# Reordering the opening, the routing stage and the last experts of a two-block transformer kernel on one Trainium2 core

## The chip, the cores and the metric

The kernel runs on one core of a Trainium2 chip. The core has five engines with queues of their own: TensorE (PE, matrix products into the eight PSUM banks), VectorE (DVE), ScalarE (ACT), GpSimd (POOL) and SyncE (SP, which here only issues DMAs). Sixteen DMA engines move data between HBM and the on-chip SBUF. Engines wait for each other through semaphores only. The metric is the device time of one execution in microseconds, lower is better.

## The reference, cut to what matters

Everything is float32. Two blocks run one after the other on 256 tokens (`x`) of width 1024; the first also carries 256 context tokens.

```python
# first block, layer 0 (gated linear attention), layer 1 (neighbourhood attention)
for i in range(2):
    mod = silu(c) @ ada_w[i] + ada_b[i]              # shifts, scales, gates
    h = rms_norm(x, g1) * (1 + s1) + sh1
    x = x + g1 * mixer(h)                            # gla_mixer or na_mixer
    h = rms_norm(x, g2) * (1 + s2) + sh2
    a, val = split(h @ w_in)                         # 1024 -> 2 * 2816
    x = x + g2 * ((silu(conv3(a)) * val) @ w_out)    # 2816 -> 1024
x = rms_norm(x, final_g)
# second block: 16 meta tokens in front of the 256
p = rms_norm(h) @ w_in_2
h = h + concat(hyena(p), hgrn2(p)) @ w_out_2
a = rms_norm(h, norm_ffn)
group = argmax(a @ w_rg); e1, e2 = top2(softmax(a @ w_re[group]))      # 64 experts
h = h + sum(gate_e * (silu(a @ w_gate[e]) * (a @ w_up[e])) @ w_down[e])
return rms_norm(h, norm_final)[16:]
```

An expert's three matrices (`w_gate`, `w_up`: 1024 x 512, `w_down`: 512 x 1024) are 2 MB each, 192 matrices in all, and the kernel reads them all.

## The kernel before, in words

**First block.** Activations lie transposed: `xT`, `hT` hold 8 chunks of 128 channels by 512 tokens (256 of them in layer 1). Weights come as slabs of 2 MB through a ring of four slots (`ring`), in an order written out in `first_block_slabs`; SP issues them one by one, each as soon as the count on the semaphore of its slot's last reader is there. The large products are split for precision: a float32 operand is rounded to the fast format `fp32r` by ACT ("hi"), DVE subtracts to get the rest ("lo"), and `split_mm` (L692 to L696) makes three fast products hi*hi, hi*lo and lo*hi in place of one plain float32 product. So each half slab passes ACT (`..._hi`), then DVE (`..._lo`, counted on `w_lo`), before PE may use it; each activation chunk passes the same way (`h_hi`, `h_lo`; in the second half of a feed-forward network `f_hi`, `f_lo`).

**Opening.** PE makes the norm's sum, then `ada_rows(0)`, `ada_rows(1)` (products of the conditioning vector with a slab of `ada_w`, 64 instructions with the four-column layout of `ada_products`), turns them (`ada_turn`) and begins the first projection: `unit(u, chunks)` adds some of the eight chunks of output tile `u`. Chunks 0 to 3 can be done once half of the modulation is known; chunks 4 to 7 need `ada_rows(2)`, `ada_rows(3)` and their turns, then DVE's `columns(1)` and ACT's `modulate`. The order on PE is: `unit(0)`, `unit(1)` with chunks 0, 1, 2; `ada_rows(2)`; chunk 3; `ada_rows(3)`; turn 2; part of `unit(2)`; turn 3; and so on. DVE does eight `factors`, then `rest(0)` and the lo half of the first weights, which POOL has rounded.

**Feed-forward, layer 1.** `ffn(l, T)` exists on PE, ACT and DVE. For 22 tiles `i` PE makes 48 products (two output halves of eight chunks, three products each). ACT rounds the weights of tile `i + 2`, does the convolution's middle tap and, after DVE's `taps`, the silu; DVE subtracts for tile `i + 2`, does the taps and the final product into `f_act`. After the loop 22 chunks of `f_act` are rounded (`ffn_out_prepared`) and subtracted (`act_rest`), the first two ahead of the rest, and eight output tiles `m` of 66 products follow, each with a slab rounded by `ffn_w_out_hi` / `ffn_w_out_lo`.

**Routing.** PE makes the logits and turns the token rows (`logits_and_rows`), waits for DVE's chain of some 25 small steps (group, two experts, ranks), makes the ranks' products (L1379 to L1382), gathers the tokens of the first expert (`gather_first`) and starts expert 0.

**Experts.** Each of the 64 experts gets 32 token slots. `expert(e)` on PE: `gate_up` (32 products of 256 columns, four side by side), a turn of the hidden tile, `down` (16 products). ACT applies silu and copies, DVE multiplies. The experts go in groups of four (`GE`); `gather` fills 128 slots for the next group, and `combine(g)` adds a finished group's rows to `z_tok`, which holds the residual, with four products of 128 x 512 and four DVE additions. `load(n)` on SP issues matrix `n` (gate, up, down of expert `n // 3`) into one of eight homes (`e_slot`) once the last reader of the home is through: for `n >= 8` the count on `gu_mm` or `down_mm`. Matrices 0 to 7 go as soon as `first_free` allows: 0 and 1 long before, 2 to 5 in the last transforms, 6 and 7 at `proj_mm` 28 and 32. Matrix 8 (`NINTH`) and matrix 9 (`TENTH`) lie in scattered free tiles (8 and 11 parts of 256 or 128 KB), after 7 in the queue. Matrices 10 and 11 share homes with 0 and 1 and are issued in quarters as expert 0's `gate_up` passes (`GU_PART`).

**The end.** After expert 63: `combine(15)`, four additions, per half of the tokens a square with a sum, Ln and Exp for the root, one DVE product with the gain, one store.

## Time and profile before

| | |
|---|---|
| runs, us | 2356.7, 2358.27, 2360.92 (median 2358.27) |
| profiled execution, us | 2357.33, of which the span from the first to the last instruction is 2355.5 |
| busy, share of the span | PE 83%, PE weight loads 62%, DVE 40%, ACT 29%, POOL 4% |
| DMA engines | 592 MB, mean 251 GB/s |
| mean granted PE clock | 0.931 of full speed |

Times in the profile are from the first instruction. A busy PE is one with a product under way, at whatever clock: the granted clock has a full level (1.00) and a half one (0.50), and a number between them is a stretch with both. A matmul in float32 that is not `fp32r` shows as two records.

### The profile page before, as it was taken

The numbers are of one execution on the slowest core, as the hardware profiler recorded it, in microseconds if no ns is written. First come the engines' busy times: TensorE is split into PE (matmuls) and PEld (weight loads), VectorE is DVE, ScalarE is ACT, GpSimd is POOL, SyncE is SP. The second block draws the span as 40 slices with busy tenths as digits, with TensorE's granted clock in tenths as the row PEclk, the third lists the DMA queues.
The fourth block names the chain that finished last, engine by engine and source line by source line (L and its number), as shares of the span: only waits on it lengthen the run. The fifth ranks groups of instructions, "written<-read, shape, count | busy, mean of one in ns | idle before, by whom it ended". The sixth has DMA issues, their size and how long they took to land.

```text
span 2355.5 us, 38024 instructions
## 1 busy us (share of the span) xinstructions
PE 1943.9 (83%) x16576; PEld 1463.5 (62%) x16576; DVE 935.4 (40%) x1636; ACT 691.0 (29%) x1255; POOL 94.2 (4%) x112
## 2 busy tenths in 40 slices
PE   5999899999999999999899998666666566666665
PEld 4896567888787887998896465433333343333332
DVE  3346745344424246665666374332111121111112
ACT  4333435322414246544553323111111111111111
POOL 0010110000001011000200000000000000000000
PEclk9999999999999999999999998888888888888888
DMA  6306462221225224444530349999999999999996
GB/s 274 144 36 245 186 250 108 107 96 61 77 107 223 108 71 173 176 162 147 215 119 10 137 198 373 426 428 427 427 427 426 428 426 427 426 428 426 427 427 279
DMA packets 47861, 592.27 MB, mean 251 GB/s; under 512 B 5917, under 2 KB 6873, under 8 KB 12240
## 3 DMA queue, kind: packets, MB, share of 16 engines
q1 hardware_dynamic: 44272, 580.21, 60.1%
q0 software_dynamic: 2992, 8.57, 1.2%
q8 instruction: 132, 2.16, 0.4%
q10 hardware_dynamic: 432, 1.06, 0.1%
q14 instruction: 33, 0.27, 0.0%
HBM read 588.77 MB, written 1.05 MB: 250 GB/s over the span
## 4 chain that ended last, share of the span: by engine, by line
PE 46%; DMA 27%; DVE 8%; ACT 5%; issue 2%; POOL 0%; SPq 0%; ACTq 0%; DVEq 0%; POOLq 0%
DMA s_ring<-in_w_up 14%; PE bank L694 9%; PE bank L696 9%; PE bank L695 9%; DMA s_arena<-in_w_up 6%; PE bank L1407 6%; DMA s_hT<-in_w_up 4%; DVE s_ring_r L2243 3%; ACT s_arena_r L1572 3%; DMA s_xT<-in_w_up 3%; PE bank L1439 2%; PE bank L1394 1%; PE bank L1445 1%; PE bank L1229 1%; ACT s_arena L1572 1%
## 5 line engine op out<-in xcount | busy, mean ns | idle before, releaser
L694 PE MATMUL bank<-s_arena_r 128*128 128x256 f32 (+2 forms) x1816 | 592.1, 326 | 24.4 <-DVE s_hT_r L2248 9.3
L696 PE MATMUL bank<-s_arena_r,s_ring_r 128*128 128x512 f32 (+2 forms) x1472 | 489.4, 332 | 0.0
L1572 ACT ACTIVATE s_arena<-bank 32x256 f32<-32x256 f32 (+6 forms) x418 | 167.5, 407 | 1025.9 <-PE bank L1407 552.8
L1407 PE MATMUL bank<-s_ring,s_arena 128*32 128x256 f32 x1984 | 279.4, 496 | 150.5 <-DMA s_hT<-in_w_up 39.6
L695 PE MATMUL bank<-s_hT_r,s_arena_r 128*128 128x512 f32 (+2 forms) x1144 | 385.1, 337 | 0.0
L694 PEld LDWEIGHTS bank<-s_arena_r 128*128 128x128 f32 x1816 | 341.2, 188 | 60.9 <-issue 13.8
L2243 DVE TENSOR_TENSOR s_ring_r<-s_ring,s_arena_r 128x2048 fp32r<-128x2048 f32 (+3 forms) x121 | 251.0, 2085 | 277.2 <-ACT s_arena_r L1572 277.0
L696 PEld LDWEIGHTS bank<-s_arena_r,s_ring_r 128*128 128x128 f32 x1472 | 278.1, 189 | 29.1
L1407 PEld LDWEIGHTS bank<-s_ring,s_arena 128*32 128x32 f32 x1984 | 135.9, 141 | 226.4 <-issue 213.9
L1572 ACT ACTIVATE s_arena_r<-s_ring 128x2048 fp32r<-128x2048 f32 (+3 forms) x121 | 208.8, 1737 | 153.3 <-PE bank L696 123.5
L2926 DVE TENSOR_TENSOR s_arena<-s_arena,bank 64x256 f32<-64x256 f32 x64 | 27.1, 423 | 522.3 <-ACT s_arena L1572 522.3
L695 PEld LDWEIGHTS bank<-s_hT_r,s_arena_r 128*128 128x128 f32 x1144 | 216.0, 189 | 24.3 <-issue 0.5
L1407 PE MATMUL bank<-s_arena 128*32 128x256 f32 x1084 | 120.4, 491 | 55.3 <-DMA s_arena<-in_w_up 37.4
L695 PE MATMUL bank<-s_arena_r 128*128 128x256 f32 (+1 forms) x464 | 150.8, 325 | 0.0
L695 PE MATMUL bank<-s_ring_r,s_arena_r 128*128 128x256 f32 (+1 forms) x464 | 130.1, 280 | 0.0
L1572 ACT ACTIVATE s_arena<-s_arena 128x512 f32<-128x512 f32 (+7 forms) x176 | 86.3, 529 | 140.2 <-DVE s_arena L2236 98.5
L1407 PE MATMUL bank<-s_hT,s_arena 128*32 128x256 f32 x544 | 92.9, 516 | 38.5 <-DMA s_ring<-in_w_up 38.5
L1407 PEld LDWEIGHTS bank<-s_arena 128*32 128x32 f32 x1084 | 62.3, 140 | 90.2 <-issue 80.7
L2984 DVE COPY s_arena<-bank 32x256 f32<-32x256 f32 x128 | 54.3, 425 | 152.1 <-PE bank L1439 149.6
L696 PE MATMUL bank<-s_arena_r,s_hT_r 128*128 128x256 f32 (+1 forms) x336 | 94.3, 281 | 0.0
L1407 PE MATMUL bank<-s_xT,s_arena 128*32 128x256 f32 x480 | 77.1, 492 | 19.6 <-DMA s_ring<-in_w_up 19.6
L695 PEld LDWEIGHTS bank<-s_arena_r 128*128 128x128 f32 x464 | 88.0, 190 | 7.3
(366 smaller groups left out, 2530.6 us busy)
## 6 DMA issues: line engine op xcount, KB each, us to landing
s_ring<-in_slabs SPq DMA_DIRECT2D x68, 2048.0 KB, 8.6
s_ring<-in_w_down SPq DMA_DIRECT2D x32, 2048.0 KB, 28.5
s_ring<-in_w_up SPq DMA_DIRECT2D x32, 2048.0 KB, 33.3
s_ring<-in_w_gate SPq DMA_DIRECT2D x30, 2048.0 KB, 33.3
s_arena<-in_w_gate SPq DMA_DIRECT2D x16, 2048.0 KB, 33.3
s_arena<-in_w_up SPq DMA_DIRECT2D x16, 2048.0 KB, 33.3
s_arena<-in_w_down SPq DMA_DIRECT2D x14, 2048.0 KB, 29.5
s_ring<-in_slabs SPq DMA_DIRECT2D x16, 1408.0 KB, 6.2
```

The lines of the kernel that those rows point to most:

```text
L694: mm(out, w_hi_, x_hi_, start=start, stop=False, skip_group_check=skip)
L695: mm(out, w_hi_, x_lo_, start=False, stop=False, skip_group_check=skip)
L696: return mm(out, w_lo_, x_hi_, start=False, stop=stop, skip_group_check=skip)
L1229: last = mm(bank[:, :], dft_w(i, kt, r0=r), (f_hs if i < 2 else f_hd)[rows, od, kt, :], start=a == 0, stop=a == 2, skip_group_check=True)
L1394: last = mm(pb[6 + hf][:, P * c:P * c + n], r_h2[:, i, 512 * hf + P * c:512 * hf + P * c + P], r_S[:, buf, i, 0:n], start=i == 0, stop=i = ...
L1407: last = mm(pb[b][32 * q:32 * q + 32, 0:256], x[:, c, :], (gate, up)[q // 2](c, q % 2), start=c == 0, stop=c == DC - 1, skip_group_check=True)
L1439: last = mm(pb[3 + b][32 * q:32 * q + 32, 0:256], e_hT[:, b, 64 * a + 32 * half_:64 * a + 32 * half_ + 32], w(2 * half_ + a, q), start=a + ...
L1445: return mm(pb[(5, 6, 7, 5)[k]][:, :], r_SgT[0:n, buf, P * i:P * i + P], y_g[0:n, buf, 512 * hf:512 * hf + 512], start=True, stop=True)
L1572: return act.activation(out, in_, func, **kw)
L2243: TTn(view_r, view, hi.bitcast(F32), ALU.subtract).then_inc(S["w_lo"], 1)
L2926: return TTn(e_hid[0:64, b, :], e_sg[0:64, b, :], pb[b][64:128, 0:256], ALU.mult)
L2984: dve.tensor_copy(y_g[32 * j:32 * j + 32, g % 2, 256 * q:256 * q + 256], pb[3 + b][32 * q:32 * q + 32, 0:256]).then_inc(S["y_dve"], 1)
```

## The change

Seven edits, in the order of the kernel.

1. **Opening.** On PE `ada_rows(2)` stands ahead of the first `unit`, `ada_rows(3)` after chunk 1, the turns after chunk 2 and 3. On DVE the lo half of the first weights stands ahead of `rest(0)`, and the last two `factors` between the rests.
2. **Feed-forward of layer 1.** The first output tile is one plain float32 product per chunk. Its chunks' hi and lo parts, for the other seven tiles, are made inside the loop of 22 (`act_rounded(i - 1)` on ACT, `act_rest(i - 2)` on DVE), in places of their own.
3. **Second block's first projection.** DVE's `half_lo(2)` stands ahead of the eight products into `zT`.
4. **Products that nobody reads** (`idle_products`, plain float32, 128 x 512): five after `ffn(1)`, five ahead of the wait for the routing (`route_M`), one after the ranks' products.
5. **Loads.** SP issues six parts of matrix 8 and two narrow ones of matrix 9 ahead of matrices 6 and 7; the first half of matrix 10 goes whole into `z_tok`, and its second half into its home.
6. **Residual.** `z_tok` is therefore not filled by ACT; the first `combined` takes the residual from `r_h2`, scaled back by `n_root`, which costs one DVE reciprocal. PE's wait for `n_act` 13 goes.
7. **Last experts.** Expert 62 runs as before; ahead of it PE puts the residual and the rows of experts 60 and 61 into four banks. Expert 63's gate and up products are 128 columns wide in 4 x 8 pieces per matrix, its up and down matrices come in halves of 1 MB with semaphores of their own, its hidden tile needs one turn. The rows of experts 62 and 63 are added by products of 32 rows (`own_rows`). Then ACT squares and DVE multiplies by the gain straight from the banks, both halves of the tokens share one Ln and one Exp, ACT scales one half, DVE the other, and both stores start together.

```diff
@@ first_block_slabs / f_hi
+            if T == NT:
+                return f_lo[:, c, NT:TT]
+        def f_rest(c, T):
+            if T == TT:
+                return f_lo[:, c, 0:T]
+            return (hT_r, xT_r, h_hi)[c // DC][:, c % DC, NT:TT]
@@ sync
+            for n in range(6):
+                load(n)
+            sp.wait_ge(S["hyena_y"], HC)
+            for i in range(6):
+                ninth_part(i)
+            narrow_part(1)
+            narrow_part(3)
+            load(6)
+            load(7)
+            sp.wait_ge(S["z_pe"], Z_ROWS(DC))
+            for i in range(6, 8):
+                ninth_part(i)
+            for i, home in enumerate(tenth_wide):
+                tenth_part(home, 512 * i)
+            narrow_part(0)
+            narrow_part(2)
+            n = TENTH + 1
+            sp.dma_start(eleventh_half, weights[n % 3][n // 3, :, 0:2048]).then_inc(S["slab_in4"], 16)
+            sp.wait_ge(S["z_set"], DC + 1)
+            for i in range(4, 6):
+                narrow_part(i)
...
                 if n == TENTH + 1:
                     for k in range(4):
-                        for i in range(2):
+                        for i in range(0 if k >= 2 else 1, 2):
...
+                if n in LAST_HALVES:
+                    sp.dma_start(e_slot[s][:, 0:2048], weights[n % 3][n // 3, :, 0:2048]).then_inc(S[LAST_HALVES[n][0]], 16)
+                    sp.dma_start(e_slot[s][:, 2048:4096], weights[n % 3][n // 3, :, 2048:4096]).then_inc(S[e_in[s][0]], 16)
+                    return
@@ tensor: ffn(l, T, norm)
+                    if m == 0 and l:
+                        w = got(out_slab(l, m))
+                        for c in range(FC):
+                            pe.wait_ge(S["ffn_act"], FC * l + c + 1)
+                            last = mm(pb[2][:, 0:T], w[:, c, :], f_act[:, c, 0:T], start=c == 0, stop=c == FC - 1)
+                        last.then_inc(S["ffn_out_mm"], 1)
+                        continue
...
+            def idle_products(bank, moving, n):
+                for _ in range(n):
+                    mm(bank[:, :], ident, moving, start=True, stop=True)
@@ tensor: opening
-            for c in range(3):
+            ada_rows(2)
+            for c in range(2):
                 unit(0, [c])
                 unit(1, [c])
-            ada_rows(2)
+            ada_rows(3)
+            unit(0, [2])
+            unit(1, [2])
+            ada_turn(2)
             unit(0, [3])
             unit(1, [3])
-            ada_rows(3)
-            ada_turn(2)
-            unit(2, range(2))
             ada_turn(3)
-            unit(2, range(2, 4))
+            unit(2, range(4))
             unit(3, range(4))
...
             ffn(1, NT, "fin")
+            idle_products(pb[0], ka[:, :], 5)
...
+            pe.wait_ge(S["route_in"], 48)
+            idle_products(pb[3], gain_out[:, 0:512], 5)
             pe.wait_ge(S["route_M"], 1)
...
+            idle_products(pb[3], gain_out[:, 0:512], 1)
...
-                pe.wait_ge(S["n_act"], 13)
@@ tensor: last_experts
+                for k, (i, hf) in enumerate(TH):
+                    mm(z_bank[k][:, :], ident, z_tok[:, i, 512 * hf:512 * hf + 512], start=True, stop=False, skip_group_check=True)
+                for k, (i, hf) in enumerate(TH):
+                    mm(z_bank[k][:, :], r_SgT[0:P - 64, 1, P * i:P * i + P], y_g[0:P - 64, 1, 512 * hf:512 * hf + 512], start=False, stop=False, skip_group_check=True)
+                expert(e - 1)
+                quarters(pb[0], arrived(3 * e), range(DC)).then_inc(S["gu_mm"], 1)
+                own_rows(0)
+                quarters(pb[3], first_half(3 * e + 1), range(4))
+                quarters(pb[3], arrived(3 * e + 1), range(4, DC)).then_inc(S["gu_mm"], 1)
+                pe.transpose(pb[2][:, 0:P], e_hid[:, 1, 0:P], ident).then_inc(S["hid_tr"], 1)
+                w = first_half(3 * e + 2)
+                for c in range(4):
+                    if c == 2:
+                        arrived(3 * e + 2)
+                    for q in range(4):
+                        last = mm(pb[4][32 * q:32 * q + 32, 0:256], e_hT[:, 1, 32 * c:32 * c + 32], w[:, D * c + 256 * q:D * c + 256 * q + 256], start=c == 0,
+                                  stop=c == 3, skip_group_check=True)
+                own_rows(1)
@@ scalar
-                    if i == FC - 1:
+                    if i == FC - 1 and l == 0:
                         ffn_w_out_hi(l, 0)
                         for c in range(2):
                             A(f_hi(c, T), f_act[:, c, 0:T], ACT.Copy).then_inc(S["f_hi"], 1)
+                    if l and i >= 1:
+                        act_rounded(i - 1)
-            for i in range(2):
-                for hf in range(2):
-                    A(z_tok[:, i, 512 * hf:512 * hf + 512], z_rows[i][hf][:, :], ACT.Copy).then_inc(S["n_act"], 1)
+                for k in range(4):
+                    act.wait_ge(S["comb_mm"], 4 * NGRP + 8 + k + 1)
+                    if k == 2:
+                        act.wait_ge(S["z_add"], 4 * (NGRP - 1) + 2)
+                    A(z_tok[:, i, 512 * hf:512 * hf + 512], z_bank[k][:, :], ACT.Square, accum_out=n_acc[:, 1, k:k + 1]).then_inc(S["n_act"], 1)
+                A(n_rstd[:, 1, :], n_rstd[:, 1, :], ACT.Ln, bias=eps[:, 0:1], scale=1.0 / D).then_inc(S["n_act"], 1)
+                A(n_rstd[:, 1, :], n_rstd[:, 1, :], ACT.Exp, scale=-0.5).then_inc(S["n_act"], 1)
+                A(r_h2[:, 1, :], r_h2[:, 1, :], ACT.Copy, scale=n_rstd[:, 1, 1:2]).then_inc(S["n_act"], 1)
@@ vector
+                    if l and i >= 2:
+                        act_rest(i - 2)
...
             factors(0, 6)
             columns(0)
-            factors(6, 2)
+            gla_w_in_lo(0)
+            rest(0)
+            rest(1)
+            factors(6, 1)
+            rest(2)
+            factors(7, 1)
+            rest(3)
...
             half_lo(1, "in2")
+            half_lo(2, "in2")
...
+                dve.wait_ge(S["n_act"], 9)
+                step(dve.reciprocal(n_root, n_rstd[:, 0, :]))
...
+                for k in (2, 3, 0, 1):
+                    TTn(r_h2[:, i, 512 * hf:512 * hf + 512], z_bank[k][:, :], gain_out[:, 512 * hf:512 * hf + 512], ALU.mult).then_inc(S["z_add"], 1)
+                TTn(n_rstd[:, 1, :], n_acc[:, 1, 0:4:2], n_acc[:, 1, 1:4:2], ALU.add).then_inc(S["z_add"], 1)
+                TS(r_h2[:, 0, :], r_h2[:, 0, :], n_rstd[:, 1, 0:1], None, ALU.mult).then_inc(S["out_set"], 1)
```

## Rows read from the trace of the kernel before

**Rows 1.** The page: GB/s in 40 slices, and the chain by engine.

```profile
GB/s 274 144 36 245 186 250 108 107 96 61 77 107 223 108 71 173 176 162 147 215 119 10 137 198 373 426 428 427 427 427 426 428 426 427 426 428 426 427 427 279
PE 46%; DMA 27%; DVE 8%; ACT 5%; issue 2%; POOL 0%; SPq 0%; ACTq 0%; DVEq 0%; POOLq 0%
```

**Rows 2.** Timeline, opening: start us, length us, engine, line, operation, count, idle before.

```profile
24.66 4.66 POOL L594 CAST s_arena_r<-s_ring 128x2048 fp32r<-128x2048 f32 x2 [23.16 <-DMA s_ring<-in_slabs]
...
32.95 0.79 PE L694 MATMUL bank<-s_arena_r 128*128 128x512 f32 x1 [7.93 <-DVE s_ring_r L2329]
...
39.83 1.95 PE L770 MATMUL bank<-s_ring,s_ones 128*32 128x128 f32 x64
...
46.74 0.27 PE L785 MATMUL bank<-s_ka,s_arena 128*128 128x128 f32 x1
```

**Rows 3.** PE's windows, opening: stretch, length, busy (count), granted clock, DMA share, GB/s.

```profile
38.00:40.00 2.00, 2.00 (x16) 0.89 1.00 426
```

**Rows 4.** Timeline, feed-forward of layer 1, all engines.

```profile
1061.30 1.90 ACT L1572 ACTIVATE s_arena_r<-s_ring 128x2048 fp32r<-128x2048 f32 x1
...
1063.23 2.29 DVE L2243 TENSOR_TENSOR s_ring_r<-s_ring,s_arena_r 128x2048 fp32r<-128x2048 f32 x1 [1.39 <-ACT s_arena_r L1572]
...
1076.88 2.77 DVE L2266 TENSOR_TENSOR s_arena_r<-s_arena,s_hT_r 128x256 fp32r<-128x256 f32 x8
...
1074.07 0.28 PE L696 MATMUL bank<-s_arena_r,s_ring_r 128*128 128x256 f32 x1
...
1088.28 0.39 PE L694 MATMUL bank<-s_arena_r 128*128 128x256 f32 x1 [3.61 <-DVE s_ring_r L2243]
```

**Rows 5.** PE's windows, in that loop and behind its stall.

```profile
1000.00:1055.00 55.00, 55.00 (x470) 1.00 0.46 167
...
1090.00:1092.00 2.00, 2.00 (x12) 0.50 0.02 6
```

**Rows 6.** Start of the second block's first projection: timeline, then chain (start, length).

```profile
1153.92 0.57 PE L694 MATMUL bank<-s_arena_r 128*128 128x272 f32 x1 [5.06 <-DVE s_hT_r L2248]
...
1168.68 0.51 DVE s_arena L2236
```

**Rows 7.** Timeline, routing and expert 0, PE and SP.

```profile
1424.08 0.79 PE L1379 MATMUL bank<-s_arena,s_ka 128*128 128x128 f32 x2 [5.07 <-DVE s_arena L2860]
...
1427.37 1.94 PE L1453 MATMUL bank<-s_arena 128*32 128x256 f32 x16 [1.32 <-DVE s_arena L2899]
...
1431.08 5.33 PE L1407 MATMUL bank<-s_arena 128*32 128x256 f32 x64 [0.54 <-ACT s_arena L1572]
...
1441.13 1.94 PE L1439 MATMUL bank<-s_ring,s_arena 128*32 128x256 f32 x32 [0.47 <-ACT s_arena L1572]
...
1443.11 0.33 SPq L560 DMA_DIRECT2D s_ring<-in_w_gate  x1
```

**Rows 8.** PE's windows of 1 us in the routing, columns as in rows 3.

```profile
1415.00:1416.00 1.00, 1.00 (x9) 1.00 0.00 0
...
1433.00:1434.00 1.00, 1.00 (x14) 0.50 0.35 121
```

**Rows 9.** PE's windows of 1 us near the end.

```profile
2319.00:2320.00 1.00, 0.29 (x4) 0.50 1.04 442
...
2331.00:2332.00 1.00, 0.00 (x0) 1.00 0.57 229
```

**Rows 10.** Timeline, the last two experts and the end.

```profile
2311.98 1.93 PE L1439 MATMUL bank<-s_ring,s_arena 128*32 128x256 f32 x32 [0.41 <-issue]
...
2334.35 0.64 PE L1407 MATMUL bank<-s_hT,s_arena 128*32 128x256 f32 x2 [4.57 <-DMA s_ring<-in_w_up]
...
2344.98 3.67 PE L1445 MATMUL bank<-s_arena 128*128 128x512 f32 x8 [1.04 <-ACT s_arena L1572]
...
2348.69 0.69 DVE L2931 TENSOR_TENSOR s_arena<-s_arena,bank 128x512 f32<-128x512 f32 x1 [0.17 <-PE bank L1445]
...
2352.47 0.36 ACTq L2174 DMA_DIRECT2D out_y<-s_arena  x1
```

More of the change, by code:

```diff
@@ L451, in build @@
         e_in = [(f"slab_in{e_ring[i]}", count[e_ring[i]]) if i in e_ring else (f"expert_in{i}", 0) for i in range(NSLOT)]
+        N_ACT = 9
+        z_bank = [pb[k] for k in (6, 7, 1, 5)]
+        own_y = [y_g[:, 0, 256 * k:256 * k + 256] for k in range(2)]
+        own_SgT = [r_SgT[:, 0, :], r_S[:, 0, :, :].rearrange("p a n -> p (a n)")]
         sems = S
@@ L1551, in _ @@
                     pe.wait_ge(S["x_done"], j + 2)
-            for e in range(GE * MIDDLE, NE):
+            for e in range(GE * MIDDLE, NE - 2):
                 expert(e)
-            combine(NGRP - 1)
+            last_experts()
         @block.scalar
```

197 lines of the change are left out of this document (142 added, 55 removed).

## The prediction

> **What bounds the kernel now.** I read the page first, then the chain of waits, then windows and timelines of the stages that the change touches. The page's GB/s line [rows 1] splits the kernel in two. Up to slice 23 (some 1390 us) the DMA rate changes from slice to slice and the chain by engine is mostly PE (46% of the span): compute is the bound. From slice 25 on the rate stands at 426 to 428 GB/s to the end: the matrices of the experts stream in, and a matrix of 2.097 MB costs 4.9 us however fast the engines are (DMA is 27% of the chain, all of it there). So a microsecond counts in four places: ahead of the stream it moves the stream's start; in the routing it counts if DMA engines have run dry; between the experts it counts nothing; behind the last matrix it counts in full.
>
> **1. Opening.** PE sits idle 7.93 us before its first projection product at 32.95 [rows 2], and the clock comes back to the full level only inside 38 to 40 (0.89) [rows 3]; the first product took 0.79 us. The turn whose result gates chunks 4 to 7 starts at 46.74 [rows 2]. The change puts `ada_rows(2)` in the hole. When is its slab there? POOL's cast, released by the third slab, starts at 24.66 [rows 2]; the fourth lands one slab later, 24.7 + 4.9 = 29.6. At half clock the 64 products take twice the 1.95 us of [rows 2], to 33.5, by when DVE has the first lo half (cast half done at 27.0, plus 2.3 [rows 4], and behind POOL's second cast, 29.3 + 2.3 = 31.6, at worst). PE works from 29.6 instead of 32.95 (3.3 us), and starts its way to full clock as much earlier: some 3.4 us less at half speed give 1.7 us. Chunks 5 and on still wait for the ACT and DVE steps behind turn 3, which move with it, so about 0.3 is lost: **4.7 us**. Bounds: 0 (the wait comes back behind the turn) and 6.5 (clock back at once).
>
> **2. Feed-forward of layer 1.** Before: the loop's last product starts at 1074.07, and the second output tile starts at 1088.28 after a wait of 3.61 us for the lo half of its weights, [rows 4]; the clock then drops to 0.50 for 3.4 us [rows 5], worth 1.7. New: behind the loop stand 22 plain products of 256 columns. The nearest row is the combine, 3.67 us for four of 512 columns plus tail [rows 10], thus 0.43 to 0.46 each, 9.7 us in all. The cover for the second tile's weights (ACT 1.90 and DVE 2.29 for 2048 columns [rows 4], so 2.6 and 3.1 for 2816) is then these 9.7 us. If the loop is as long as before, tile 1 starts at 1074.2 + 9.7 = 1083.9, a gain of 4.4.
> But the loop gets a longer chain. ACT's rounding (1.90), DVE's subtraction (2.29, starting 1.9 after it) [rows 4], the taps, the silu and the return to ACT make a ring of 5.5 us per tile (1.9 + 2.3 + two taps of 0.5, [rows 6], + 0.3). PE needs 48 x 55/470 = 5.62 [rows 5], only 0.1 more. `act_rest(i - 2)` stands in this ring between the subtraction and the taps and costs 2.77 / 8 = 0.35 [rows 4]; 17 tiles of it are 5.9 us. ACT's extra rounding lies beside DVE's subtraction and is free. The cover: tile 21's lo half is ready at 1063.23 + 2.29 = 1065.5, PE needs it at 1074.2 - 5.6 = 1068.6, so 3.1 us are spare and PE slips by 5.9 - 3.1 = 2.8. Gain: 4.4 - 2.8 + 1.7 (no stall, no clock drop) = **3.3 us**. Bounds: 6.1 (no slip), and -2 (ACT's step of the same size in the ring too).
>
> **3. Second block's projection.** The unread products (5 x 0.86 = 4.3 us by [rows 10]) lie in a wait of 5.06 us [rows 6]. PE then begins at full clock, but is paced by DVE's h_lo, and the fifth tile waits for DVE's taps of the first (second tap at 1168.68, [rows 6]). Moving `half_lo(2)` ahead of the eight products leaves the taps behind the same sum of DVE work. **0**; bounds -1 (a product at half clock sticks out) and +1.4.
>
> **4. Routing and loads.** Before: DMA ran dry at 1415 (0 GB/s) and partly at 1433 (121) [rows 8], because matrices 6 and 7 wait for PE and the quarters of 10 and 11 for expert 0. The first free-running matrix, 12, is issued at 1443.11 [rows 7], when expert 0's `down` is through; by then what was queued is just delivered. From issue to flow lie some 1.7 us: matrix 12 starts to arrive at 1444.8.
> New: the parts of 8 and 9 (1.8 MB, 4.3 us) fill the time behind matrix 5; half of 10 (2.5 us) fills the hole before the quarters. All twelve matrices are in some 2 us before matrix 12 can flow (the three megabytes left of 10 and 11 take 7.4 us from about 1431.6 on). But then matrix 12 decides, which waits for `down_mm` 1, so what counts is how much sooner PE is through with expert 0. PE waits 5.07 us for DVE's routing chain [rows 7], during which the clock goes to half and stays there at 1433 [rows 8]. Five products (4.3 us at full clock, from 1419.0 to 1423.3) lie in that wait with 0.8 to spare. With the clock held, the ranks' product (0.79) saves 0.3, the gather (1.94) 1.0, the turn 0.25, expert 0's 5.33 goes to 8 x 0.43 = 3.4 (four columns of 256 side by side, the combine's rate in [rows 10]), 1.9; the 4.7 us from there to its `down` were at full clock already [rows 7]. Sum 3.45, so **3.5 us**: matrix 12 at 1439.6 instead of 1443.1, its data flowing from 1441.3 instead of 1444.8. The reciprocal (0.2) lies beside PE's gathers. Bounds: if the clock drops all the same but after the five, 0.5; if it drops under them (5 x 1.7 = 8.5 us, 3.4 more than the wait), -3.1; 6 if PE gives more.
>
> **5. Last experts.** Before: matrix 190 (up) releases PE at 2334.35, at half clock after 4.57 us idle; `combine` starts at 2344.98, the last addition at 2348.69, the last store at 2352.47, and the end is 3.0 us behind it [rows 10]. New: gate products of expert 63 are done while 190 lands; of 190 only half a matrix of products is left (0.9 to 1.7 us). Matrix 191's second half lands 4.9 us after 190, at 2339.2, and is now what ends last. From there: 8 of 16 down products 1.0, copy 0.45, eight products of 32 rows in two turns 1.3, a ladder of ACT squares and DVE products on two banks each 2.8 (4 x 0.69 [rows 10]), sum, Ln and Exp 0.8, scaling 1.2: 2346.8. Then 3.0 and, as both 0.5 MB stores start together, 1.2 more (0.5 MB at the 427 GB/s of [rows 1]): 2351.0. Against 2355.5: **4.5 us**. Bounds: 2 (32-row products one after the other, 8 x 0.43) and 6 (stores beside each other, squares closer).
> By the Trainium skill, "DMA: Bandwidth & Descriptors", section "Issuing engines are not separate DMA queues", DMAs started by two engines end up on the same 16 engines and interleave. The row for one store shows 3.0 us to the end; no row has two together. By that rule the 1.2 stand; without it the sum would be 1.2 better.
> The extra work ahead of expert 62 (16 small and 8 large products, 8 us) starts at 2313.9, and expert 62's matrix lets PE start at 2319.7 [rows 9, 10]: 2.5 us late, but then at full clock. Its cover is the wait for 190; were it gone (all at half clock) the end would move by up to 2 us.
>
> **Sum.** 4.7 + 3.3 + 0 + 3.5 + 4.5 = 16.0. The profiled execution took 2357.33 us (span 2355.5 and 1.8 around it), which is 0.9 below the median of the runs, 2358.27. 2357.33 - 16.0 = 2341.3; with half of that difference added, I say **2341.8**.
>
> **Rivals.**
> A. *The clock is not held in the routing.* Between the products PE still has four waits of 0.5 to 1.3 us [rows 7]. For: the clock was at half through all such waits before. Against: it had fallen in the long one ahead. Time: item 4 at 0.5 or -3.1, thus 2344.8 to 2348.4. The Trainium skill, "TensorE: Matmul & The Clock Gate", section "A second HAM failure mode: psum-queue depth-cycling", says that short idle stretches between groups of matmuls make the clock swing; by it this rival comes true. The trace shows the granted clock at 1.00 at 2331 after a `down` with waits around it [rows 9], which speaks against it.
> B. *The ring of layer 1 does not reach PE,* or half as much: 2339.0. For: no PE wait in the loop [rows 5]. Against: the spare time counted above.
> C. *Tail or opening give half:* 32-row products in series, or PE waiting again behind the third turn. 2344.2.
> D. *Slower.* In the last 12 us the engines move only 229 GB/s [rows 9]: about half of the sixteen are through and half are behind by some 12 us in a stream of 950 us, and the late half sets every landing. If parts with short rows in a new order, or the halves, put more on the late half, the stream itself stretches. It decides from 16/950 = 1.7%; at 2% it costs 19 us: 2361. For: the lag exists. Against: all changed transfers together are under 10 MB of 403, and rate in all slices is the same.
> E. *The front's gain is eaten* by a wait in the attention stages: only items 4 and 5 count, 2349.8.
>
> **How the numbers follow.** Forecast 0.47, A 0.20, B 0.12, C 0.10, D 0.05, E 0.06. A change of 0.2% (4.7 us) is about what a measurement of this kernel can tell: faster means below 2353.6. All but D are there; for errors in several items at once I take some off: faster 0.88, same 0.07, slower 0.05. The range reaches to A and B with their bounds: 2334 to 2350.
>
> **What would show it.** PE's `ada_rows(2)` at 29 to 30 and turn 3 near 42; in layer 1 small PE waits for lo halves from about tile 9 on, and tile 1 without the 3.61 us wait; PE clock 1.00 at 1420 to 1430; matrix 12 issued 3 to 4 us earlier relative to the routing; the last store issued some 8 us behind the last matrix's landing instead of 13. Wrong if turn 3 moves and the scan does not, or if the slices from 25 on show less than 426 GB/s.

## The result and the profile after

| | before | after |
|---|---|---|
| median of the runs shown side by side, us | 2356.81 (2354.54 to 2360.92) | 2342.97 (2340.68 to 2348.44) |
| ratio | | 0.9942, 95% interval 0.9933 to 0.9952 |
| profiled execution, us | 2357.33 | 2340.68 |
| its span, us | 2355.5 | 2338.9 |
| mean granted clock | 0.931 | 0.938 |

The forecast was 2341.8 us, in a range of 2334 to 2350. The interval lies clear of 1: the kernel is faster by 0.6%. The gain itself is known less well than the table suggests. The span of the profiled execution is 16.6 us shorter, where the sum of the five terms said 16.0, but that execution was the fastest of its six; the two medians lie 13.8 us apart, and in the sets of runs below the changed kernel is 17.9 and 16.2 us ahead.

The page of the changed kernel, the GB/s line and the chain by engine, answers to [rows 1]:

```profile
GB/s 276 145 37 261 183 241 109 108 103 55 78 108 224 110 69 176 158 167 163 207 129 10 125 207 394 426 427 427 428 426 427 427 426 427 428 426 427 427 427 311
PE 48%; DMA 29%; DVE 6%; ACT 4%; issue 2%; POOL 0%; SPq 0%; DVEq 0%; ACTq 0%; POOLq 0%
```

The shape is the same: compute up to slice 23, the stream of expert matrices at 426 to 428 GB/s from slice 25 on. The slice between them rose from 373 to 394 GB/s. So the stream did not stretch (rival D); it starts earlier, has fewer holes at its start, and less comes behind it.

**Opening.** Timeline of the changed kernel (start us, length us, engine, line, operation, count, idle before), against [rows 2]:

```profile
24.43 4.16 POOL L625 CAST s_arena_r<-s_ring 128x2048 fp32r<-128x2048 f32 x2 [22.93 <-DMA s_ring<-in_slabs]
26.79 3.94 DVE L2492 TENSOR_TENSOR s_ring_r<-s_ring,s_arena_r 128x2048 fp32r<-128x2048 f32 x1
30.55 3.64 PE L812 MATMUL bank<-s_ring,s_ones 128*32 128x128 f32 x64 [5.95 <-DMA s_ring<-in_slabs]
34.12 0.61 PE L725 MATMUL bank<-s_arena_r 128*128 128x512 f32 x1
37.19 1.95 PE L812 MATMUL bank<-s_ring,s_ones 128*32 128x128 f32 x64
42.06 0.27 PE L827 MATMUL bank<-s_ka,s_arena 128*128 128x128 f32 x1
```

`ada_rows(2)` fills the hole, at half clock (3.64 us; its twin at 37.19 takes 1.95), and turn 3 (`ada_turn(3)`, the one that gates chunks 4 to 7) stands at 42.06 where it was at 46.74. The slab landed 0.9 us later than I had it. DVE's lo half takes 3.94 us beside POOL's cast; the same operation takes 2.28 us at 34.40, where POOL is idle.

**Feed-forward of layer 1 and the projection behind it**, against [rows 4] and [rows 6]:

```profile
1064.26 2.29 DVE L2399 TENSOR_TENSOR s_ring_r<-s_ring,s_arena_r 128x2048 fp32r<-128x2048 f32 x1 [1.39 <-ACT s_arena_r L1690]
1066.47 0.42 DVE L2422 TENSOR_TENSOR s_arena_r<-s_arena,s_arena_r 128x256 fp32r<-128x256 f32 x1
1072.37 9.66 PE L763 MATMUL bank<-s_arena,s_ring 128*128 128x256 f32 x44
1140.62 4.45 PE L784 MATMUL bank<-s_ka 128*128 128x512 f32 x10
1145.84 0.36 PE L725 MATMUL bank<-s_arena_r 128*128 128x272 f32 x1 [0.76 <-DVE s_hT_r L2404]
1153.73 0.40 PE L725 MATMUL bank<-s_arena_r 128*128 128x272 f32 x1 [1.64 <-DVE s_ring_r L2399]
```

The plain tile takes 9.66 us (22 products, recorded as 44), the wait of 3.61 us behind it is gone. The projection begins 8.08 us earlier than in [rows 6], 4.65 of which the opening gave.

**Routing**, against [rows 7]:

```profile
1410.78 0.34 PE L1420 MATMUL bank<-s_ka,s_arena 72*128 72x72 f32 x2 [0.25 <-ACT s_arena L1690]
1410.96 4.50 PE L784 MATMUL bank<-s_arena,s_ka 128*128 128x512 f32 x10
1416.18 0.49 PE L1425 MATMUL bank<-s_arena,s_ka 128*128 128x128 f32 x2 [0.72 <-DVE s_arena L3025]
1421.50 3.66 PE L1454 MATMUL bank<-s_arena 128*32 128x256 f32 x64 [0.43 <-ACT s_arena L1690]
1422.62 1.19 SPq L546 DMA_DIRECT2D s_arena<-in_w_down  x2
1431.86 0.33 SPq L561 DMA_DIRECT2D s_ring<-in_w_gate  x1
```

Windows of it, against [rows 8] (stretch, its length, busy us of PE, PEld, DVE, ACT, POOL, granted clock, DMA share, GB/s):

```profile
1407.00:1408.00 1.00, 1.00 (x10) 0.93 (x10) 0.03 (x1) 0.00 (x0) 0.00 (x0) 1.00 1.03 442
1425.00:1426.00 1.00, 1.00 (x12) 0.91 (x9) 0.97 (x4) 0.38 (x1) 0.00 (x0) 1.00 1.01 356
```

The two stretches that stood at 0 and 121 GB/s carry 442 and 356, the clock is full, expert 0's gate and up products take 3.66 us instead of 5.33, and matrix 12 is issued 21.08 us behind the 72 x 72 turn instead of 24.44. The first of the quarters of matrices 10 and 11 (the row of L546) is issued 11.84 us behind it.

**The end**, against [rows 10]:

```profile
2325.38 1.07 PE L1633 MATMUL bank<-s_xT,s_arena 128*32 128x256 f32 x16 [0.46 <-ACT s_arena L1690]
2327.04 1.07 PE L1633 MATMUL bank<-s_xT,s_arena 128*32 128x256 f32 x16 [0.59 <-DMA s_xT<-in_w_down]
2328.71 1.56 PE L1604 MATMUL bank<-s_arena 32*128 32x256 f32 x16 [0.60 <-ACT s_arena L1690]
2330.38 2.57 DVE L3235 TENSOR_TENSOR s_arena<-bank,s_arena 128x512 f32<-128x512 f32 x4 [1.77 <-PE bank L1604]
2333.82 0.75 DVE L3239 TENSOR_SCALAR s_arena<-s_arena 128x1024 f32<-128x1024 f32 x1 [0.60 <-ACT s_arena L1690]
2334.99 0.37 ACTq L2330 DMA_DIRECT2D out_y<-s_arena  x1
```

Only half of the down products (1.07 us) are left when the last bytes arrive, and the last store is issued 8 us behind that release. By the trace's DMA records the last packet of the weights ends at 2326.55, 8.4 us ahead of the last store and 12.3 us ahead of the end; in the kernel before it ended at 2338.66, 13.8 us and 16.9 us ahead of them.

### The profile page after: what moved, and what is told of

Read it like the earlier page. It is cut to its first block, busy times and chain, and to the rows that moved or that the text cites. A ratio compares the mean times of both kernels' runs of the same rounds, so it can differ in the third digit from the quotient of the medians.

```text
span 2338.9 us, 38292 instructions
## 1 busy us (share of the span) xinstructions
PE 1953.3 (84%) x16711; PEld 1466.6 (63%) x16711; DVE 929.9 (40%) x1634; ACT 687.8 (29%) x1253; POOL 93.7 (4%) x112
## 4 chain that ended last, share of the span: by engine, by line
PE 48%; DMA 29%; DVE 6%; ACT 4%; issue 2%; POOL 0%; SPq 0%; DVEq 0%; ACTq 0%; POOLq 0%
DMA s_ring<-in_w_up 14%; PE bank L725 10%; PE bank L727 10%; PE bank L726 10%; DMA s_arena<-in_w_up 6%; PE bank L1454 5%; DMA s_xT<-in_w_up 4%; DMA s_hT<-in_w_up 3%; DVE s_ring_r L2399 2%; ACT s_arena_r L1690 2%; PE bank L1490 2%; DMA s_xT<-in_w_down 1%; PE bank L1441 1%; PE bank L1273 1%; PE bank L1496 1%
## 5 line engine op out<-in xcount | busy, mean ns | idle before, releaser
L725 PE MATMUL bank<-s_arena_r 128*128 128x256 f32 (+2 forms) x1858 | 603.5, 325 | 8.5 <-DVE s_hT_r L2404 3.9
L727 PE MATMUL bank<-s_arena_r,s_ring_r 128*128 128x256 f32 (+2 forms) x1514 | 499.4, 330 | 0.0
L726 PE MATMUL bank<-s_hT_r,s_arena_r 128*128 128x512 f32 (+2 forms) x1200 | 398.9, 332 | 0.0
L1454 PE MATMUL bank<-s_ring,s_arena 128*32 128x256 f32 x1952 | 272.3, 494 | 146.9 <-DMA s_hT<-in_w_up 39.4
L725 PEld LDWEIGHTS bank<-s_arena_r 128*128 128x128 f32 x1858 | 347.6, 187 | 46.4 <-issue 9.1
L726 PEld LDWEIGHTS bank<-s_hT_r,s_arena_r 128*128 128x128 f32 x1200 | 225.0, 188 | 24.2 <-issue 0.5
L1690 ACT ACTIVATE s_arena<-s_arena 128x512 f32<-128x512 f32 (+6 forms) x174 | 85.1, 527 | 137.9 <-DVE s_arena L2392 96.0
L1454 PE MATMUL bank<-s_hT,s_arena 128*32 128x256 f32 x512 | 85.9, 509 | 34.3 <-DMA s_ring<-in_w_up 34.3
L726 PE MATMUL bank<-s_arena_r 128*128 128x512 f32 (+1 forms) x330 | 112.5, 341 | 0.0
L726 PEld LDWEIGHTS bank<-s_ring_r,s_arena_r 128*128 128x128 f32 (+1 forms) x464 | 85.9, 185 | 0.5
```

What stands on the lines that cost most here:

```text
L725: mm(out, w_hi_, x_hi_, start=start, stop=False, skip_group_check=skip)
L726: mm(out, w_hi_, x_lo_, start=False, stop=False, skip_group_check=skip)
L727: return mm(out, w_lo_, x_hi_, start=False, stop=stop, skip_group_check=skip)
L1454: last = mm(pb[b][32 * q:32 * q + 32, 0:256], x[:, c, :], (gate, up)[q // 2](c, q % 2), start=c == 0, stop=c == DC - 1, skip_group_check=True)
L1690: return act.activation(out, in_, func, **kw)
```

## The experiments

The kernels ran in three sets, each on a chip of its own and beside runs of the kernel before. Sets 1 and 3 hold the changed kernel too, as a yardstick. Set 2 (residual ahead, opening held, old end, old opening) has none, and "above the yardsticks" there compares runs on different chips; the medians of the kernel before were 2359.09, 2356.70 and 2357.65 us in the three sets. Times are medians of five. Single executions of one kernel lie up to 8 us apart (2340.68 to 2348.44 for the changed kernel), and the intervals of most kernels overlap that of the yardstick, so a difference of 2 or 3 us between two medians decides nothing alone. I read each verdict from lengths of stages inside the traces as well, one trace per kernel:

| kernel | median us | ratio to before, interval | turn 3 | norm sum | to projection | turn 72x72 to matrix 12 | to last half |
|---|---|---|---|---|---|---|---|
| changed, set 1 | 2341.24 | 0.9932 (0.9919 to 0.9946) | 41.47 | 938.18 | 206.81 | 21.10 | 915.47 |
| changed, set 3 | 2341.50 | 0.9934 (0.9920 to 0.9948) | 41.94 | 938.82 | 206.82 | 21.09 | 916.63 |
| no products in routing | 2345.34 | 0.9942 (0.9929 to 0.9956) | 43.06 | 937.95 | 206.91 | 24.50 | 921.18 |
| old loads | 2344.49 | 0.9942 (0.9929 to 0.9956) | 41.85 | 938.16 | 207.43 | 21.09 | 918.48 |
| neither | 2346.30 | 0.9953 (0.9940 to 0.9967) | 41.63 | 938.48 | 206.87 | 24.47 | 920.65 |
| residual ahead | 2338.70 | 0.9929 (0.9915 to 0.9942) | 42.12 | 937.71 | 204.57 | 21.09 | 916.31 |
| opening held | 2341.53 | 0.9935 (0.9921 to 0.9948) | 40.07 | 936.23 | 206.80 | 21.09 | 918.03 |
| old end | 2345.04 | 0.9947 (0.9934 to 0.9961) | 41.70 | 938.37 | 206.89 | 21.09 | |
| old opening | 2347.67 | 0.9964 (0.9950 to 0.9977) | 46.87 | 943.64 | 206.89 | 21.09 | 916.57 |
| old feed-forward | 2345.57 | 0.9951 (0.9938 to 0.9965) | 42.15 | 937.51 | 210.24 | 21.08 | 916.37 |
| item 3 off | 2341.56 | 0.9938 (0.9925 to 0.9952) | 41.71 | 938.49 | 206.83 | 21.09 | 916.12 |
| both gains | 2336.71 | 0.9913 (0.9900 to 0.9927) | 40.10 | 934.81 | 203.95 | 21.09 | 915.95 |

"Turn 3" is the start of `ada_turn(3)` in the opening, "norm sum" the start of PE's sum ahead of the second block's feed-forward, "to projection" the time from there to the first product of the second block's projection, "to last half" from PE's 72 x 72 turn in the routing to the product that the last matrix's second half releases (the old end has no halves). All lengths are in us.

### The changed kernel as yardstick (two runs)

No edit.

> The changed kernel itself, unedited, as the yardstick for the runs beside it. Every theory: 2341 to 2346 us, 14 to 16 us under the kernel before.

> The changed kernel itself once more, as the yardstick of the three runs beside it. Every theory: 2340 to 2345 us.

Measured: 2341.24 and 2341.50 us.

### No products in the routing

```diff
-            pe.wait_ge(S["route_in"], 48)
-            idle_products(pb[3], gain_out[:, 0:512], 5)
...
-            idle_products(pb[3], gain_out[:, 0:512], 1)
```

> The six unread products in the routing are left out (five behind the group product, one ahead of the first expert), all loads stay as changed. Theory T (the routing part of the gain needs PE's clock held, because PE's last products there say when the quarters of matrices 11 and 12 and later matrix 12 may be issued): the granted clock falls from 1.00 to 0.50 in about 1418 to 1424, matrix 12 is issued 2.5 to 3.7 us later than in the changed kernel (1431.9), and the kernel takes 2 to 4 us more. Rival (DMA alone counts, the early loads give all of it): within 0.7 us of the changed kernel.

Measured: 2345.34 us, 4.1 above the yardstick. Timeline and two windows of this kernel:

```profile
1415.01 0.80 PE L1423 MATMUL bank<-s_arena,s_ka 128*128 128x128 f32 x2 [5.07 <-DVE s_arena L3022]
1421.89 5.49 PE L1451 MATMUL bank<-s_arena 128*32 128x256 f32 x64 [0.43 <-ACT s_arena L1687]
1423.88 2.04 SPq L546 DMA_DIRECT2D s_arena<-in_w_down  x2
1434.09 0.33 SPq L561 DMA_DIRECT2D s_ring<-in_w_gate  x1
```

```profile
1419.00:1420.00 1.00, 1.00 (x12) 0.20 (x4) 0.18 (x1) 0.00 (x0) 0.00 (x0) 0.50 1.15 450
1424.00:1425.00 1.00, 1.00 (x16) 0.61 (x12) 0.86 (x6) 0.00 (x0) 0.00 (x0) 0.50 0.55 94
```

The wait of 5.07 us of [rows 7] is back, the clock stands at 0.50 behind it, and expert 0's gate and up products take 5.49 us (5.33 in [rows 7], 3.66 in the changed kernel). Behind the turn the first quarter is issued 2.5 us later (14.29 us) and matrix 12 3.4 us later (24.50), and as the early loads are then through, the queues run low (94 GB/s). The rival, that DMA alone gives the gain, is out.

### Loads in the old order

```diff
-            for n in range(6):
+            for n in range(8):
                 load(n)
...
-            n = TENTH + 1
-            sp.dma_start(eleventh_half, weights[n % 3][n // 3, :, 0:2048]).then_inc(S["slab_in4"], 16)
```

The counts of the waits, the four quarters of the eleventh matrix and `up` of expert 3 go with it.

> The six products stay; the loads go back to the order of before (matrices 6 and 7 ahead of the ninth's and tenth's parts, no half of the eleventh in the residual's buffer, four quarters of it into its slot). Theory T (early loads are needed too, since otherwise the queues run dry and the stream is short of 1 MB when PE could go on): the DMA share falls to about 0 for 1 to 2 us near 1407, PE waits for the eleventh or twelfth matrix, and the kernel takes 1.5 to 3.5 us more than the changed one. Rival H (the clock alone is the gain, the bytes were there in any case): within 0.7 us of the changed kernel.

Measured: 2344.49 us, 3.3 above. Window of this kernel:

```profile
1407.00:1408.00 1.00, 1.00 (x9) 0.85 (x9) 0.26 (x1) 0.00 (x0) 0.00 (x0) 1.00 0.00 0
```

Matrix 12 is issued at the same 21.09 us behind the turn as in the changed kernel, and still 1.8 us of the stream are lost (counted in bytes, below): the dry microseconds can't be made up. The rival "clock alone" is out. My expectation had PE waiting for the eleventh or twelfth matrix; no such wait exists. The lost bytes come out only at the end of the stream. The median's 3.3 is more than the loss: in the profiled execution of this kernel the work behind the last bytes took 14.2 us and not 12.3, with its last products at half clock (see the last section); some kernels with the new loads show the same.

### Neither

Both edits together.

> Both left out: no products held in the routing and the loads in the order of before. Theory T (two conditions, of which the later one counts): 3 to 4.5 us more than the changed kernel, clearly less than the sum of what the two single edits cost if each of these costs over 2 us. Rival S (the two gains add): the sum of the two single edits' costs, 5 us or more.

Measured: 2346.30 us, 5.1 above, a little more than I expected; the two single costs sum to 7.4. To count it inside the traces I took the bytes of the 69 us that start exactly 34 us ahead of the 72 x 72 turn, and set them against 427 GB/s. (The start must be exact: nothing flows there yet, so a window that starts 0.4 us earlier counts 0.4 us more as lost.) Time lost: changed kernel 7.5 (set 1), 7.7 (set 3) and 7.9 us; no products 11.8; old loads 9.5; neither 12.1; kernel before 12.2. Against the mean of the changed kernel, 7.7, the single edits cost 4.1 and 1.8, both together 4.4, and the routing term is worth 4.3 us between the two profiled executions of before and after. From there to 2303 us the stream loses 0.1 to 0.4 us in all of them. It's two conditions of which the later one counts; they don't add: with the new loads the products are worth 4.1 us, with the old ones 2.6, and the loads alone 0.3. "Neither" still has item 6, which no run takes out; the kernel before, without it, loses the same.

### Activation residual ahead of the weight's

```diff
+                    if l and i >= 2:
+                        act_rest(i - 2)
                     if i + 2 < FC:
                         ffn_w_in_lo(l, i + 2)
...
-                    if l and i >= 2:
-                        act_rest(i - 2)
```

> In the second block's feed-forward loop VectorE makes the activation's residual of two chunks ago ahead of the weight's residual instead of behind it, in the 1.39 us that it idles there. Theory R (the ring of VectorE and ScalarE sets the period of 5.83 us, because the 0.44 us of residual stand behind the wait): the period goes back to 5.5, the first plain product stands 2 to 3 us earlier than the 1072.5 of the changed kernel, and the kernel is 2 to 3.2 us faster. Rival P (PE sets the period, or the residual delays the weight's residual that PE needs): within 0.7 us.

Measured: 2338.70 us. That is 2.7 below the yardsticks, but they belong to other sets; against the kernel before beside it the ratio is 0.9929, where the yardsticks have 0.9932 and 0.9934, which would be 1 us. So the median does not decide, and the stage does. Timeline of this kernel, the last tile of the loop with a weight's residual:

```profile
1056.43 0.42 DVE L2422 TENSOR_TENSOR s_arena_r<-s_arena,s_arena_r 128x256 fp32r<-128x256 f32 x1
1057.90 2.29 DVE L2399 TENSOR_TENSOR s_ring_r<-s_ring,s_arena_r 128x2048 fp32r<-128x2048 f32 x1 [1.05 <-ACT s_arena_r L1690]
1068.79 9.66 PE L763 MATMUL bank<-s_arena,s_ring 128*128 128x256 f32 x44
```

The residual stands in DVE's idle time now. DVE's weight residuals follow each other every 5.50 us, as in the kernel before, and not every 5.83 us as in the changed kernel. From the norm sum to the plain tile it is 131.1 us instead of 133.3, and 130.5 in the kernel with both gains, where no clock drop falls in the loop's start. PE counts 469 matmul records in 1000 to 1055, against 454 in the changed kernel and 470 in [rows 5]: the ring no longer reaches PE. The slip that the prediction put at 2.8 us is 2.2 to 2.8. The expectation holds, rival P is out.

### Products in the opening's wait

```diff
+            idle_products(pb[3], ka[:, 0:512], 6)
             ada_rows(2)
```

> Six unread products of 128x512 (0.89 us each at full clock) stand in the opening in PE's 5.95 us wait for the slab, ahead of the adaLN group's product. Theory (a granted clock of 0.50 in 28 to 34 costs that group 3.64 instead of 1.95 us): clock 1.00 throughout 24 to 36, the group takes 1.95 us, turn 3 at about 40.4 instead of 42.1, and the kernel is 1.2 to 1.9 us faster. Rival (behind the group PE waits for ScalarE and VectorE, which are busy in 26 to 34): the first product of the unit stays near 34.1, and nothing or under 0.5 us is gained. Other rival: the six products end behind the slab's landing and cost their overhang, up to 0.5 us slower.

Measured: 2341.53 us. Timeline of this kernel:

```profile
24.64 5.32 PE L784 MATMUL bank<-s_ka 128*128 128x512 f32 x12
30.26 1.96 PE L812 MATMUL bank<-s_ring,s_ones 128*32 128x128 f32 x64 [0.31 <-DMA s_ring<-in_slabs]
40.07 0.27 PE L827 MATMUL bank<-s_ka,s_arena 128*128 128x128 f32 x1
```

The opening does what the theory says: turn 3 comes 1.4 to 1.9 us sooner, and the routing 2.0 to 2.6 us. The time does not show it. In the profiled execution the engines trickle on at 0.02 to 0.24 of their share in the last 4 us of the stream, the last half is released 1.4 to 2.6 us late, and its products run at half clock (1.93 us instead of 1.07), with 14.2 us from the last bytes to the end instead of 12.3. By itself this run is inconclusive.

### The end as before

Everything that item 7 adds is taken out: `expert(62)`, `expert(63)`, `combine(15)`, the old additions, squares and scaling.

```diff
-            for e in range(GE * MIDDLE, NE - 2):
+            for e in range(GE * MIDDLE, NE):
                 expert(e)
-            last_experts()
+            combine(NGRP - 1)
```

> Everything of the change but the last two experts, which run as before: no halves of the last two matrices, products of 32 rows for all, combination of 128 rows after the last down product, squares and scaling after the additions. The term of the prediction: 4.5 us (2 to 6) slower than the changed kernel, 17 us or more from the last byte of the weights to the end of the span against 12.9. Rival (the end of the stream comes later by itself, the tail is hidden by the lag of some DMA engines): under 2 us.

Measured: 2345.04 us, 3.7 above the mean of the yardsticks. The span is 2343.9 us and the last packet of the weights ends at 2326.96, so 16.9 us lie behind it, as in the kernel before, against 12.3 in the changed kernel (2338.9 and 2326.55). The difference is 4.6 us. Windows of both, first the changed kernel, then this one, and the timeline of this one:

```profile
2326.50:2327.00 0.50, 0.00 (x0) 0.00 (x0) 0.00 (x0) 0.00 (x0) 0.00 (x0) 1.00 0.00 0
2326.50:2327.00 0.50, 0.50 (x12) 0.30 (x8) 0.00 (x0) 0.00 (x0) 0.00 (x0) 0.50 0.00 0
```

```profile
2333.36 3.67 PE L1491 MATMUL bank<-s_arena 128*128 128x512 f32 x8 [1.04 <-ACT s_arena L1619]
2337.07 0.69 DVE L2999 TENSOR_TENSOR s_arena<-s_arena,bank 128x512 f32<-128x512 f32 x1 [0.17 <-PE bank L1491]
```

The two long steps of [rows 10] are back with the same lengths. The rival is out. Five of the twelve traces with the new end have the last products at half clock and 14.2 us behind the last bytes; against those the new end is worth 2.7 us and not 4.6.

### The opening as before

The order of PE and DVE of before:

```diff
-            ada_rows(2)
-            for c in range(2):
+            for c in range(3):
                 unit(0, [c])
                 unit(1, [c])
-            ada_rows(3)
...
+            ada_rows(2)
```

> Everything of the change but the order of the opening stage, which is the order of before on PE and VectorE. The term of the prediction: turn 3 back at 46.7, kept to the end, 4.7 us (3.5 to 5.5) slower than the changed kernel. Rival E (a later stage takes part of a gain at the front): under 3 us slower.

Measured: 2347.67 us, 6.3 above the yardsticks. Turn 3 at 46.87, the norm sum at 943.64, as in the kernel before (46.74, 943.71); against the yardsticks 4.8 to 5.5 us. It's the largest term, and kept to the end. Rival E is out. The median's 6.3 is above my 5.5; in this profiled execution the last half of the stream is released 4.9 to 6.7 us later than in the yardsticks, so the rest is scatter of the executions and of the sets as far as I can tell.

### The second feed-forward as before

The plain tile, the rounding in the loop and the places of the residuals are taken out, for `l` = 1 all runs as for `l` = 0.

```diff
-                    if m == 0 and l:
-                        w = got(out_slab(l, m))
...
-                    if l and i >= 2:
-                        act_rest(i - 2)
```

> Everything of the change but the second block's feed-forward, which is made as before (first output tile with three products per chunk, activation rounded behind the loop). The term of the prediction: from the norm sum ahead of the loop to the second block's projection 3.3 us longer than in the changed kernel, with PE waiting 3.6 us before the second tile and the clock at 0.50 beside it, and the kernel 3.3 us (2.5 to 4.5) slower. Rival (the slip of the ring and the plain tile cancel): under 1.5 us slower.

Measured: 2345.57 us, 4.1 above; 210.24 to the projection, 3.4 more. Timeline and window of this kernel:

```profile
1082.10 0.38 PE L721 MATMUL bank<-s_arena_r 128*128 128x256 f32 x1 [3.61 <-DVE s_ring_r L2382]
```

```profile
1084.00:1086.00 2.00, 2.00 (x11) 2.00 (x11) 1.44 (x2) 0.53 (x2) 0.00 (x0) 0.50 0.00 0
```

The wait of 3.61 us is back to the hundredth and the clock stands at 0.50 behind it: the term's 3.3 us. The rival is out.

### Item 3 off

```diff
-            idle_products(pb[0], ka[:, :], 5)
...
-            half_lo(2, "in2")
```

> Left out: the five unread products behind the second feed-forward; and the weight's residual 2 of the input projection is made inside its loop again, as before. The prediction puts this item at nothing (-1 to 1.4): within 0.7 us of the changed kernel, although the granted clock may stand at 0.50 for some us near 1140 to 1146. Rival: a projection tile at half clock moves all behind it, 0.7 to 1.5 us slower.

Measured: 2341.56 us, the same as the yardsticks, and 206.83 to the projection. Timeline and window of this kernel:

```profile
1145.32 0.56 PE L725 MATMUL bank<-s_arena_r 128*128 128x272 f32 x1 [5.05 <-DVE s_hT_r L2403]
```

```profile
1147.00:1149.00 2.00, 2.00 (x11) 2.00 (x10) 2.00 (x7) 1.27 (x4) 0.00 (x0) 0.50 0.00 0
```

The projection starts at half clock, as before the change, and nothing is later for it: from the norm sum to the 72 x 72 turn of the routing it is 471.63 us, and 471.59 in the yardstick. In the changed kernel PE's next wait there, at 1153.73, is for DVE. The rival is out.

### Both gains

The edits of "residual ahead" and "opening held" in one kernel.

> The changed kernel with both edits that helped one by one: VectorE's activation residual ahead of the weight's residual, and six unread products in PE's opening wait. If the two lie in stages of their own, the gains add: the routing starts 2.5 + 2 = 4.5 us earlier than in the changed kernel, and the time is 3.5 to 5 us below it, about 2338 us. Rival (the stream of weights starts at a fixed time or ends no earlier): less than half of that.

Measured: 2336.71 us, 4.8 below the yardstick beside it, and 0.9913 of the kernel before. Timeline of this kernel:

```profile
40.10 0.27 PE L827 MATMUL bank<-s_ka,s_arena 128*128 128x128 f32 x1
1403.44 0.34 PE L1421 MATMUL bank<-s_ka,s_arena 72*128 72x72 f32 x2 [0.25 <-ACT s_arena L1691]
2319.39 1.07 PE L1634 MATMUL bank<-s_xT,s_arena 128*32 128x256 f32 x16 [1.39 <-DMA s_xT<-in_w_down]
```

The routing starts 7.0 us earlier than in the yardstick of its set (1410.41). The edits account for 1.8 + 2.9 of it, where I expected 2.5 + 2, so the two gains add and the rival is out. Some 2.3 us come from clock drops between 240 and 300 us that fell on other instructions (below), which is luck of this one execution. The stream from the turn to the last half is as long as ever. It's the fastest version of this study.

## Why the prediction was right, point by point

**Where luck helped.** The forecast 2341.8 is 1.2 us off the median 2342.97. It started from a median of the kernel before, 2358.27, that is 1.5 us above the one beside the result, so by medians the gain came out at 13.8 us where the forecast had 16.5. The other two sets give 17.9 and 16.2. What follows compares single traces, stage by stage.

**Term 1, opening: 4.7 said, 4.65 to 5.5 measured.** The trace gives 4.65 (norm sum at 939.06 against 943.71), the reversed order costs 4.8 to 5.5. The pieces were off in opposite ways. The slab landed at 30.5 and not 29.6, so PE works 2.4 us earlier and not 3.3. The full clock came back at 34.4 instead of 38.5, 4.1 us earlier and not 3.4, which is worth 2.0 and not 1.7. And none of the 0.3 us that I took off for the steps behind turn 3 was lost. By the Trainium skill, "SBUF — State Buffer", section "Terms", VectorE and GpSimd share a port pair and the one that waits is blocked; the trace agrees: DVE's lo half takes 3.94 us and ends at 30.73, 2.1 us after POOL's second cast, where it takes 2.28 us with POOL idle. That is the case that I called the worst (31.6), and it costs nothing: PE is busy with `ada_rows(2)` until 34.2.

**Term 2, feed-forward: 3.3 said, 3.4 measured.** The tile takes 9.66 us (9.7). The slip is 2.8 (2.8): DVE's ring went from 5.50 to 5.83 us per tile (0.33, where I had 0.35), and moving one line took it away. The old feed-forward brings back the wait and the half clock behind it, for which I had 1.7. One sign that I named did not show: small PE waits from tile 9 on. PE is busy 54.88 of 55 us in 1000 to 1055; the slip is only seen in the count of products (454 against 470) and in DVE's period. Rival B is out.

**Term 3: 0 said, 0 measured.**

**Term 4, routing and loads: 3.5 said, 4.3 measured.** The clock was held and PE got faster by what I said: matrix 12 is issued 3.36 us sooner behind the turn (3.45 said) and falls back by that without the products. What failed in part is the step from there to the stream, "then matrix 12 decides". Timeline and window of the kernel before:

```profile
1433.06 0.33 SPq L549 DMA_DIRECT2D s_arena<-in_w_up  x1
1443.00:1444.00 1.00, 1.00 (x28) 0.71 (x22) 0.90 (x4) 0.75 (x2) 0.00 (x0) 1.00 1.03 422
```

When matrix 12 was issued there (1443.11), the engines were moving 422 GB/s from what was still queued, and no hole follows. The hole of 121 GB/s at 1433 lies ahead of the quarters of matrices 10 and 11, of which the first was issued at 1433.06, 14.39 us behind the turn. In the changed kernel it is 11.84 us. So the held clock first brings the quarters sooner, by 2.55 us; of all kernels only the one without products runs low again at matrix 12 (295 to 377 GB/s from 25 to 32 us behind the turn). The other part are the dry stretches ahead of the turn, which I took for covered because what is queued is through before matrix 12 anyway: the run with the old loads shows that they cost 1.8 us at an unchanged issue time. That 3.5 is near 4.3 is thus partly luck. The 1.7 us from issue to flow, which I gave no row for, stand in no run either: the first packets of matrix 12's size (16 KB) start 2.3 us behind its issue in the kernel before and 1.1 us in the changed one.

Rival A is out, although PE waits seven times for another engine, for 0.25 to 0.81 us, between 1409 and 1446: the granted clock is 1.00 in every microsecond of it. It falls in the one wait of 5.07 us (to 0.50 at 1420.9 in the kernel before). The Trainium skill, "TensorE: Matmul & The Clock Gate", section "A second HAM failure mode: psum-queue depth-cycling", tells of a kernel whose clock goes back and forth because PE idles briefly between groups of products; this stretch does not show it.

**Term 5, last experts: 4.5 said, 4.5 measured** in the traces (16.9 us behind the last bytes against 12.3) and 3.7 by the medians. Where the last products fall at half clock, as in five of twelve traces, it is 2.7; I had not priced that. From the release by the last half to the last store I had 7.55 us, it is 7.95; from there to the end 4.2, it is 3.9. Two stores of 0.5 MB together end 0.9 us later than one behind the other did; I took 1.2.

**The sum.** 4.65 + 3.4 + 0 + 4.3 + 4.5 = 16.9 against 16.6 us of span; of the 0.3 us, 0.2 were lost between the projection and the routing (264.94 us against 264.75). The costs of the reversals by medians (6.3, 4.1, 0.2, 5.1, 3.7) sum to 19.4 and are the rougher measure: each carries the scatter of two medians. Rival E is out with the opening's shift of 4.65 still there at 939; C with terms 1 and 5.

## What to carry to other kernels

Ask of each saved microsecond in which place it lies. In this kernel: ahead of a DMA-bound stretch it moves the start, inside it nothing, behind it all counts. Where two conditions release the same transfer, price both alone and together, and expect about the larger, not the sum (4.1 and 1.8 gave 4.4 here). And where an engine has idle time ahead of a wait in a ring, an added instruction belongs ahead of that wait: 0.42 us per tile cost 2.8 us in all behind it and nothing ahead of it.

## What the runs showed of the hardware that I had not expected

**The place of a clock drop moves between executions and is worth 1 to 2 us.** The same 64 products of an adaLN group (the modulation's products with a slab) in three traces. First the changed kernel in the yardstick of set 3, timeline and window:

```profile
285.96 3.23 PE L812 MATMUL bank<-s_ring,s_ones 128*32 128x128 f32 x64 [0.51 <-DVE s_mods L2610]
287.00:288.00 1.00, 1.00 (x28) 1.00 (x22) 0.33 (x1) 0.00 (x0) 0.00 (x0) 0.50 0.00 0
```

Then the changed kernel in the execution of the result:

```profile
287.31 1.96 PE L812 MATMUL bank<-s_ring,s_ones 128*32 128x128 f32 x64
```

Then the kernel with both gains:

```profile
283.42 1.95 PE L812 MATMUL bank<-s_ring,s_ones 128*32 128x128 f32 x64
281.00:282.00 1.00, 0.97 (x4) 0.25 (x5) 0.96 (x3) 0.00 (x0) 0.00 (x0) 0.50 0.00 0
```

The granted clock falls to 0.50 after short products and waits in all three, but it stands there from 286.5 to 289.9 in the first, from 280.1 to 287.0 in the second and from 279.4 to 282.9 in the third, so it catches the group or misses it. The first two are the same kernel. The same holds at the very end: the last half of the last down products took 1.07 us in seven executions of kernels with the new end and 1.93 to 1.94 in five. From the last bytes to the end it was 12.3 us in six of the seven (13.3 in the yardstick of set 1) and 14.2 in the five. What decides which of the two comes, no run here tells.

**The stream's end scatters, not its rate.** Between 1446 and 2303 us each kernel loses 0.1 to 0.4 us against 427 GB/s, but the last 10 to 12 us run at about half the rate, with a DMA share of 0.5 to 0.6, and the last half was released 915.5 to 918.0 us behind the turn in kernels with the same routing. That half of the engines is through by then and half lags, as the prediction has it, fits the share but is not shown by it. What decides the lag I have not tried.

**Products of 32 rows in different row groups run beside each other.** Eight of them with 256 columns (recorded as 16) take 1.56 us, 0.2 each, where 256 columns of a 128-row product in [rows 10] took 0.43 to 0.46. They run in two turns of four, each in another row group and bank, and the four of a turn start within 0.02 us of each other in the trace.
